# Reserved bytes in SBUF that shift where the operands of the split products begin

## The reference

```
z = jnp.einsum('bsd,dc->bsc', rms_norm(x, norm1_g), w_in)
...
merged = gm[:, :, 0] * (y_nsa @ w_up_nsa) + gm[:, :, 1] * (y_dil @ w_up_dil)
x = x + merged.astype(x.dtype) @ w_o
x = x + peer(rms_norm(x, norm2_g), peer_wq, peer_subkeys, peer_u, peer_v)
```

```
merged = gates[:, :, 0] * y_a + gates[:, :, 1] * y_b + gates[:, :, 2] * y_c
x = x + rms_norm_2(merged @ w_o, n_post_mix)
gu = rms_norm_2(x, n_pre_ffn) @ w_ffn_gu
ffn = (jax.nn.silu(gu[..., :D_FF]) * gu[..., D_FF:]) @ w_ffn_down
return x + rms_norm_2(ffn, n_post_ffn)
```

## Time and profile before

| | |
|---|---|
| median of 3 runs | 3966.41 us (3957.11 to 3966.58) |
| span of the profiled execution | 3964.4 us |
| PE busy | 3753.1 us, 95% |
| PEld busy | 3179.7 us, 80% |
| DVE, ACT, POOL busy | 2372.2, 1446.9, 400.2 us |
| mean granted TensorE clock | 0.960 of full speed |
| mean DMA traffic | 151 GB/s |

### The profile page before, as it was taken

The page is one execution under the profiler, slowest core; times in us unless marked ns, Lnnn a source line. Parts: engine busy times, 40 slices in busy tenths (PEclk is TensorE's granted clock), DMA queues, the critical chain, the costliest instruction groups (busy, mean ns, idle before and its releaser), DMA issues. The chain is left out here.

```text
span 3964.4 us, 48266 instructions
## 1 busy us (share of the span) xinstructions
PE 3753.1 (95%) x18325; PEld 3179.7 (80%) x18325; DVE 2372.2 (60%) x4316; ACT 1446.9 (36%) x2496; POOL 400.2 (10%) x305
## 2 busy tenths in 40 slices
PE   8999999999999989999999988999999898999998
PEld 6667777799999989999977767868877676777886
DVE  3363445478999978888844455554334545555433
ACT  3232234333389934333323223332222322333221
POOL 0010000000024434333200010000000001000000
PEclk9989798999999989999999899999999999999999
DMA  3221113255589999999822223322232222332332
GB/s 129 77 69 32 30 43 99 85 163 176 172 285 379 378 373 358 383 366 368 323 84 86 59 76 93 134 78 91 92 94 80 70 77 67 107 114 85 96 91 69
DMA packets 212362, 597.91 MB, mean 151 GB/s; under 512 B 21730, under 2 KB 79748, under 8 KB 210596
## 3 DMA queue, kind: packets, MB, share of 16 engines
q1 hardware_dynamic: 175268, 460.58, 35.1%
q0 software_dynamic: 36864, 134.23, 8.8%
HBM read 525.00 MB, written 69.21 MB: 150 GB/s over the span
## 5 line engine op out<-in xcount | busy, mean ns | idle before, releaser
L364 ACT ACTIVATE stream_hi<-stream_raw 128x1024 fp32r<-128x1024 f32 (+1 forms) x615 | 642.5, 1045 | 1230.1 <-PE ffn_ps L2470 435.4
L372 DVE TENSOR_TENSOR stream_lo<-stream_raw,stream_hi 128x1024 fp32r<-128x1024 f32 (+1 forms) x615 | 745.2, 1212 | 447.3 <-ACT stream_hi L364 439.2
L942 PE MATMUL experts_ps<-mix_a_hi,stream_hi 128*128 128x384 f32 x1024 | 345.3, 337 | 19.3 <-issue 17.7
L400 PE MATMUL experts_ps<-h_hi,stream_hi 128*128 128x384 f32 x1024 | 349.5, 341 | 1.5 <-PEq L101 1.5
L942 PE MATMUL experts_ps<-mix_a_hi,stream_lo 128*128 128x384 f32 x1024 | 345.0, 337 | 0.0
L942 PE MATMUL experts_ps<-mix_a_lo,stream_hi 128*128 128x384 f32 x1024 | 345.0, 337 | 0.0
L400 PE MATMUL experts_ps<-h_lo,stream_hi 128*128 128x384 f32 x1024 | 344.8, 337 | 0.0
L400 PE MATMUL experts_ps<-h_hi,stream_lo 128*128 128x384 f32 x1024 | 344.7, 337 | 0.0
L2468 PE MATMUL mid_ps<-h_hi,stream_hi 128*128 128x512 f32 x672 | 288.6, 429 | 20.1 <-DVE h_lo L2497 17.1
L2468 PE MATMUL ffn_ps<-h_hi,stream_hi 128*128 128x512 f32 x704 | 287.5, 408 | 17.7 <-DVE h_lo L2497 17.7
L2469 PE MATMUL ffn_ps<-h_lo,stream_hi 128*128 128x512 f32 x704 | 279.7, 397 | 0.0
(11 more groups left out here) (456 smaller groups left out, 7438.1 us busy)
## 6 DMA issues: line engine op xcount, KB each, us to landing
stream_raw<-u SPq DMA_DIRECT2D x128, 512.0 KB
stream_raw<-v SPq DMA_DIRECT2D x128, 512.0 KB
stream_raw<-l_gu SPq DMA_DIRECT2D x88, 512.0 KB
expert_hidden<-experts_gelu SPq DMA_DIRECT2D x128, 192.0 KB
expert_weights<-built SPq DMA_DIRECT2D x12, 2048.0 KB
built<-expert_weights SPq DMA_DIRECT2D x16, 1536.0 KB
built<-expert_hidden SPq DMA_DIRECT2D x128, 192.0 KB
stream_raw<-l_gate SPq DMA_DIRECT2D x48, 512.0 KB
```

The source lines that it names most:

```text
L364: self.nc.scalar.activation(self.hi[n % self.RING][:, 0:w], self.raw[n % self.RAW][:, 0:w], ACT.Copy).then_inc(self.hi_done, 1)
L372: self.nc.vector.tensor_tensor(self.lo[n % self.RING][:, 0:w], self.raw[n % self.RAW][:, 0:w], self.hi[n % self.RING][:, 0:w].bitcast(F32) ...
L400: mm = self.nc.tensor.matmul(self.ps[n % 2], a, b[:, k, :], start=(k == 0 and m == 0), stop=(k == DC - 1 and m == 2))
L942: mm = nc.tensor.matmul(out[d][:, DIRECT:SEQ], v, a[b % RING][:, :], start=(b == 0 and m == 0), stop=(b == KEYS - 1 and m == 2))
```

## The change

Four tensors are added that nothing reads or writes; they only hold places of 192, 224, 160 and 224 bytes a partition.

```
 def layers(nc, A, x, C, gains2, gate_dram, stream, out):
     with ExitStack() as base:
         right = lambda name, shape, dt=F32: base.enter_context(nc.sbuf_tensor(name, shape, dt, side="right"))
+        right("right_place", [P, 56])
+        base.enter_context(nc.sbuf_tensor("left_place", [P, 40], F32))
...
         with Stage(nc, "stream") as st:
+            st.sb("ring_place", [P, 48], side="right")
             stream = Stream(nc, st, first_pieces(A) + expert_pieces(A) + layer_pieces(A))
...
                     C2.cos2, C2.sin2 = (st.sb(n, [P, SEQ], side="right") for n in ("cos2", "sin2"))
+                    place.enter_context(nc.sbuf_tensor("next_place", [P, 56], F32, side="right"))
                     next_hi, next_lo = (place.enter_context(nc.sbuf_tensor(n, [P, DC, SEQ], F32R, side="right"))
```

## The result

The changed kernel takes 3918.19 us (median of four runs, 3917.26 to 3921.93) against 3966.49 us before; the ratio is 0.9887, with a 95% interval of 0.9872 to 0.9903. That is 48.3 us less, where 30 us were forecast.

The account below looks back on a forecast made before the run. PE, busy for 95% of the span, was taken as the bound. Steps 1 to 3 (20.2, 9.7 and 1.7 us) sum to 31.6 us, less 4% 30 us, taking 3966.4 to 3937 us; full range 3926 to 3970 us.

Parts of the forecast that it names:

- What bounds the kernel: Whole kernel: PE is busy for 95% of the span, so time is saved only where PE's own stream gets shorter.
- ACT and DMA do not become late: Feed-forward and layers: ACT's waits up to 4.6 us far exceed 0.1 us shortening a piece; DMA busy 28% in layers.
- Rival D: Experts' output stage tips over to DMA if the ring's new place slows loads: up to 27 us added; chance 0.03.
- the rule of 16-byte lines: SBUF accesses pay when crossing to a new 16-byte line; by it alone the kernel would stay at 3966 us.
- Rival B: Dense products: the 4 to 5 ns belong to the stages, addresses do nothing; no change, 3966 us; chance 0.11.
- Rival C: Ring matmuls: gain is there, but stationary start at 32 costs 2 ns each, 27 us; about 3963 left; chance 0.06.
- Steps 1 and 2: Layers' moving operands to 32: next and h 4704 x 4.3 ns, 20.2 us; merge_y, latent_c, ffn_a 1872 x 5.2 ns, 9.7 us.
- step 3: Ring from 224 to 32: 384 matmuls where it moves gain 4.3 ns, 1.7 us; where stationary, nothing counted.
- the 4%: Taken off the 31.6 us sum, leaving 30 us, because matmuls in the layers' time at 1.2 GHz get no gain.
- rival A: All matmuls: moving less stationary start modulo 256 decides, not place; 22 to 29 us slower, 3988 to 3995 us; chance 0.14.
- Step 4: First block's and experts' moving operands stay at 32, so (296 x 3) + 6144 matmuls gain nothing.

Follow-up runs that it names:

- all_at_0: Against the kernel before: placeholders put the ring and all moving operands at 0 past a multiple of 256 bytes; 3919.75 us, ratio 0.9893.
- shift_256: Control against the kernel before: 256-byte placeholders ahead of the ring and the layers' left side, remainders and distances unchanged; 3965.60 us, ratio 1.0005.
- ring_only: Against the kernel before: ring moved to 32, moving operands left where they were (32, 192, 128); 3962.42 us, ratio 0.9997.
- moving_only: Against the kernel before: all moving operands at 32, ring left at 224; 3939.08 us, ratio 0.9944.
- the first sweep: Separate small kernel of matmuls alone, 8 moving by 8 stationary starts; 544 to 562 cycles for 512 columns, 416 to 424 for 384, by distance.
- distance_96: Against the kernel before: placeholders put the ring at 0 and every moving operand at 96; 3979.11 us, ratio 1.0033.

## Why the prediction was wrong

*What bounds the kernel* held: only PE's spacing changed, and all of it reached the time. *ACT and DMA do not become late*: held, and all_at_0 and shift_256 show that moving the operands of DVE, ACT and DMA costs the kernel's time nothing that the runs can tell. Rival D did not happen: from the first L942 to the first matmul of the layers it took 545.7 us before, 545.3 in ring_only, 545.0 in all_at_0 and 548.1 after the change, and 547.9 in moving_only, where the ring did not move. The Trainium skill's page "SBUF — State Buffer", section "Door 1: The DMA port swizzle", states the rule of 16-byte lines, from which the prediction worked out that contiguous operands which begin a line cost the same. That doesn't hold: the first sweep has 544 to 562 cycles among such starts. Rival B fell with ring_only, which changes the layers' and the first block's spacing with no other difference. Rival C fell with the changed profile: with the stationary start at 32 the dense products are at 226.7 ns and the experts still at 173.3.

*Steps 1 and 2*, 229.0 ns in place of 233.3 and 234.2 for 6576 matmuls: right for the moving side alone, as moving_only shows (228.8 ns, 3939 us). For the whole change they came out at 226.7 ns.

*The step that failed is step 3*, "where it is stationary, which is nearly everywhere, I count nothing", and with it the reading that the place of the moving operand decides. Moving the ring took 2.3 ns more, 229.0 to 226.7, off 6576 matmuls of the layers and the queries and 1224 of the first block: 7800 x 2.3 = 17.9 us, 17 less the 4%, of the 18 us by which the forecast fell short. The step had itself named 4.3 ns more as the best case, 28 us for the 6576 alone, but the range did not go down to the 3910 us or so that follow. What decides is rival A's distance. I had set A aside since "distances 224 and 192 give the same 233.3 to the tenth, which a collision should not". The table shows that four of eight distances share 560 cycles: equal costs at two points were no evidence against a dependence. And I had priced A at 233.3 ns, the ordinary value, when the one distance that no row showed was the best of all. So the forecast's mechanism was wrong and its amount a part of the truth, and the rival's mechanism right and its sign wrong. That the direction came out right was luck: no row of before showed distance 0.

*Step 4*, nothing for what stays at 32: the first block gained 2.3 ns a matmul with the ring. It also counted 888 matmuls where there are 1224, since up_y and up_m (112 x 3) were left out. The experts gained nothing, as stated, but for another reason: at 384 columns the distances 64 and 0 cost the same 416 cycles.

The sum with the table's values: 4704 x 6.7 = 31.4 us, 1872 x 7.5 = 14.0, the moving ring 2.2 (288 at 6.6 ns, 96 with every fourth token at 2.8), the 1224 products of 512 columns in the first block that stay at 32 x 2.3 = 2.8. Together 50.4, less the same 4% for the lower clock: 48 us. Measured: 48.3. The 4% is an estimate, so that they agree this closely is partly chance.

*What 4% for the clock was worth*: fair for the medians. No distance that is seen at 1.2 GHz costs anything there: the dense products are 427 ns apart before, after and in distance_96 alike. In the two profiles the layers' stretches gave 36.7 us against 44 due, with 11 us more of their time at 1.2 GHz after the change (159 against 148), while the first block up to up_y, with 10 us less of it, gave 6.1 us in place of 3 (888 products at 2.3 ns, and 192 of the moving ring).

## What to carry to other kernels

Where matmuls with float32r operands of 512 columns run densely, let moving and stationary tiles start at the same remainder modulo 256 bytes; it costs a few placeholders of under 256 bytes each and was worth 1.1% here, while a bad distance cost 0.3%. With 384 columns distance 0 is as good as any and 32, 96, 128 and 192 are worse. Other formats were not tried. Check spacing, not the duration column, and look for several values of one instruction form at one clock. And where the change goes to a point that no row shows, carry a rival in each direction of that point: an unseen value of a periodic cost is not the average of the seen ones.

## What the runs showed that was not expected

A contiguous stream of 512 columns at 2.4 GHz took 544 cycles at best, 32 more than its columns, and 384 columns took 416, again 32 more, while at 1.2 GHz the spacing is 427 ns, the 512 columns alone, in the kernel at distances 0, 64, 96 and 224 alike. The cost of a distance has lasting rhythms (gaps of 226, 227, 227 ns at distance 0; 229, 232, 226 at 64; 232, 235 at 224), and a single odd start 160 bytes further disturbs three or four matmuls. At 256 columns distance 0 is not the best: 288 cycles against 282 at 160.
